# The first RMSNorm's gains: one row spread by TensorE in place of a 128-partition load, and a new order of the opening steps

## The reference

```python
def rms_norm(x, g):
    x32 = x.astype(jnp.float32)
    y = x32 * lax.rsqrt(jnp.mean(x32 * x32, axis=-1, keepdims=True) + EPS)
    return (y * g.astype(jnp.float32)).astype(x.dtype)

def reference(x, norm_mix_g, w_in, ...):
    h = x
    for layer in range(DEPTH):
        hn = rms_norm(h, norm_mix_g[layer])
        h = h + hybrid_mixer(hn, w_in[layer], ...)     # z = hn @ w_in first
        hn = rms_norm(h, norm_ffn_g[layer])
        h = h + swiglu(...) if layer % 2 == 0 else h + moe_swiglu(...)
    return rms_norm(h, final_g)
```

## Time and profile before

| | us |
|---|---|
| median of 3 runs | 2067.91 (2066.62 to 2069.62) |
| profiled execution, whole time | 2069.79 |
| its span | 2068.1 |
| PE busy | 2014.9 (97%) |
| DVE busy | 1539.8 (74%) |
| ACT busy | 1202.7 (58%) |
| POOL busy | 96.7 (5%) |

### The profile page before, as it was taken

The page is one execution under the profiler, slowest core; times in us unless marked ns, Lnnn a source line. Parts: engine busy times, 40 slices in busy tenths (PEclk is TensorE's granted clock), DMA queues, the critical chain, the costliest instruction groups (busy, mean ns, idle before and its releaser), DMA issues.

```text
span 2068.1 us, 33621 instructions
## 1 busy us (share of the span) xinstructions
PE 2014.9 (97%) x11091; PEld 1748.2 (85%) x11092; DVE 1539.8 (74%) x1705; ACT 1202.7 (58%) x1546; POOL 96.7 (5%) x142
## 2 busy tenths in 40 slices
PE   8999999999999998999999999999999999999996
PEld 7777888888888777999899988888999888889995
DVE  6896766666668976766577688898776798997774
ACT  4443555555555333655465577787655687876661
POOL 1000000100000002100000000000000000001010
PEclk9999999999999998999999999999999999999998
DMA  7321776766643313877587699999877799999771
GB/s 223 120 72 47 223 219 202 218 197 190 185 143 123 112 71 103 275 236 234 204 273 253 196 360 377 357 394 353 288 254 245 278 388 357 388 356 360 258 254 41
DMA packets 245272, 487.51 MB, mean 236 GB/s; under 512 B 16724, under 2 KB 86468, under 8 KB 245220
## 3 DMA queue, kind: packets, MB, share of 16 engines
q1 hardware_dynamic: 237668, 462.04, 66.1%
q0 software_dynamic: 7552, 24.80, 3.4%
HBM read 473.21 MB, written 13.58 MB: 235 GB/s over the span
## 4 chain that ended last, share of the span: by engine, by line
PE 82%; DVE 9%; issue 3%; DMA 3%; ACT 2%; POOL 0%; DVEq 0%; SPq 0%; ACTq 0%; POOLq 0%
PE PS L1575 81%; DMA raw<-in_expert_w 2%; DVE PS L894 2%; DVE wlo L753 2%; ACT whi L375 1%; DVE OV L868 1%; DVE OV L882 1%; PE PS L1903 1%; PE PS L1605 0%; DVE OV L898 0%; DVE OV L864 0%; PE PS L1827 0%; DMA OV<-in_norm_mix_g 0%; DMA OV<-x_tok,idx 0%; DMA raw<-in_w_in 0%
## 5 line engine op out<-in xcount | busy, mean ns | idle before, releaser
L753 DVE TENSOR_TENSOR wlo<-raw,whi 128x1024 fp32r<-128x1024 f32 x872 | 1031.9, 1221 | 201.8 <-ACT whi L375 195.9
L375 ACT ACTIVATE whi<-raw 128x1024 fp32r<-128x1024 f32 x872 | 888.0, 1053 | 255.5 <-PE PS L1575 155.9
L1575 PE MATMUL PS<-XN,whi 128*128 128x512 f32 (+3 forms) x3328 | 953.5, 363 | 15.1 <-issue 9.7
L1575 PE MATMUL PS<-XN,wlo 128*128 128x152 f32 (+3 forms) x2944 | 775.3, 263 | 1.0 <-issue 1.0
L1575 PEld LDWEIGHTS PS<-XN,whi 128*128 128x128 f32 x3328 | 618.7, 189 | 81.6 <-issue 17.5
L1575 PE MATMUL PS<-whi,XN 128*128 128x512 f32 x2272 | 672.5, 394 | 7.1 <-issue 2.2
L1575 PEld LDWEIGHTS PS<-XN,wlo 128*128 128x128 f32 x2944 | 561.9, 191 | 12.8
L1575 PEld LDWEIGHTS PS<-whi,XN 128*128 128x128 f32 x2272 | 424.5, 188 | 102.3 <-issue 6.9
L1575 PE MATMUL PS<-wlo,XN 128*128 128x512 f32 x1248 | 425.0, 392 | 0.0
L1575 PEld LDWEIGHTS PS<-wlo,XN 128*128 128x128 f32 x1248 | 234.7, 188 | 50.8
L587 ACT ACTIVATE OV<-PS 128x352 f32<-128x352 f32 x112 | 51.5, 461 | 107.8 <-PE PS L1575 107.8
(11 more groups left out here) (248 smaller groups left out, 991.6 us busy)
## 6 DMA issues: line engine op xcount, KB each, us to landing
raw<-in_expert_w SPq DMA_DIRECT2D x672, 512.0 KB, 5.1
raw<-in_ffn_w SPq DMA_DIRECT2D x144, 512.0 KB, 3.8
raw<-in_w_in SPq DMA_DIRECT2D x40, 512.0 KB, 5.4
raw<-in_w_out SPq DMA_DIRECT2D x16, 512.0 KB, 4.3
y_rows<-OV POOLq DMA_DIRECT2D x13, 512.0 KB, 4.8
y_rows<-OV POOLq DMA_DIRECT2D x13, 192.0 KB, 5.1
RES<-in_x SPq DMA_DIRECT2D x4, 512.0 KB, 5.5
x_tok<-OV POOLq DMA_DIRECT2D x4, 512.0 KB, 2.9
```

The source lines that it names most:

```text
L375: act.activation(whi[:, u0 % CONV, half(h)], raw[:, r, half(h)], ACT.Copy).then_inc(s["hi_done"], 1)
L753: dve.tensor_tensor(wlo[:, w, half(h)], raw[:, u0 % RAW, half(h)], whi[:, w, half(h)].bitcast(F32), ALU.subtract).then_inc(s["lo_done"], 1)
L1575: return pe.matmul(out_, lhsT, rhs, start=start, stop=stop, skip_group_check=True)
```

## The change

- The gains of the first norm are no longer loaded into 128 partitions by SP. ACT, as its first instruction, issues a DMA of the single 4 KB row into partition 0 of `OV` (`g_row`). TensorE multiplies a row of ones with it, twice 512 columns, into banks 2 and 3 of PSUM (`gB0`), and raises `gB0_ok`. `scaled` reads `gB0` from PSUM for the first four blocks.
- TensorE's first fillers wait for `bd_zero` 3 (the third POOL constant, `ones`) in place of `const_ok`; they multiply `ones` by `ones`. The two spreading matmuls stand behind them.
- The scratch of the four first `squares` moves from PSUM banks 0 to 3 to SBUF (`sq` and the old place of `gB`), and the wait for `ss_done` 4 ahead of the second fillers is gone. These are 20 fillers now, where 14 were.
- ACT: `squares(3)` moves behind the two halves of unit 0.
- DVE: `scaled(2)` moves from ahead of `x_lo(0)` to behind the split of the second weight half, and `scaled(3)` to between the halves of unit 1.

```diff
+        g_row = OV[0:1, 3072:4096]
+        gB0 = PS[:, 2:4, :].rearrange("p a n -> p (a n)")
@@ SP
                 sp.dma_start(RES[:, b, :], x[0, b * P:(b + 1) * P, :]).then_inc(s[f"x{b}"], 16)
-                if b == 1:
-                    sp.dma_start(gB, norm_mix_g[0].partition_broadcast(P)).then_inc(s["gB0_in"], 16)
@@ ACT
+            act.dma_start(g_row, norm_mix_g[0:1, :]).then_inc(s["gB0_in"], 16)
             act.wait_ge(s["small_ok"], 3)
@@ ACT start_norm
-                for b in range(TB):
+                def first_squares(b):
+
                     act.wait_ge(s[f"x{b}"], 16)
-                    squares(b, PS[:, 2 * (b % 2):2 * (b % 2) + 2, :].rearrange("p a n -> p (a n)"))
-                for h in range(2):
-                    x_hi(h)
-                    split(0, 0, 0, (h,))
+                    squares(b, gB if b % 2 else sq.rearrange("p c n -> p (c n)"))
+
+                for b in range(TB - 1):
+                    first_squares(b)
+                x_hi(0)
+                split(0, 0, 0, (0,))
+                x_hi(1)
+                split(0, 0, 0, (1,))
+                first_squares(TB - 1)
                 split(1, 0, 0)
@@ DVE scaled, start_norm
-                dve.scalar_tensor_tensor(x_home(n), RES[:, n % TB, :], SM[:, 40 + n:41 + n], gB, ALU.mult,
-                                         ALU.mult).then_inc(s["xt_done"], 1)
+                dve.scalar_tensor_tensor(x_home(n), RES[:, n % TB, :], SM[:, 40 + n:41 + n], gB0 if n < TB else gB,
+                                         ALU.mult, ALU.mult).then_inc(s["xt_done"], 1)
                 mean(0)
-                dve.wait_ge(s["gB0_in"], 16)
+                dve.wait_ge(s["gB0_ok"], 1)
                 scaled(0)
-                for n in (1, 2):
-                    mean(n)
-                    scaled(n)
-                for h in range(2):
-                    x_lo(h)
-                    split(0, 0, (h,))
+                mean(1)
+                scaled(1)
+                mean(2)
+                x_lo(0)
+                split(0, 0, (0,))
+                x_lo(1)
+                split(0, 0, (1,))
                 mean(3)
+                scaled(2)
+                split(1, 0, (0,))
                 scaled(3)
-                split(1, 0)
+                split(1, 0, (1,))
@@ TensorE mixer(0)
-                    pe.wait_ge(s["const_ok"], 1)
-                    keep_busy(10, 6)
+                    pe.wait_ge(s["bd_zero"], 3)
+                    for _ in range(10):
+                        mm(PS[:, 6, 0:P], ones[:, :], ones[:, :], True, True)
+                    pe.wait_ge(s["gB0_in"], 16)
+                    for h in range(2):
+                        ins = mm(gB0[:, 512 * h:512 * h + 512], ones[0:1, :], g_row[:, 512 * h:512 * h + 512], True, True)
+                    ins.then_inc(s["gB0_ok"], 1)
                     x_T(0, 0)
                     x_T(0, 1)
-                    pe.wait_ge(s["ss_done"], TB)
-                    keep_busy(14, 3)
+                    keep_busy(20, 0)
                 pe.wait_ge(s["xlo_done"], 8 * l + 2)
```

2 lines of the change are left out of this document (1 added, 1 removed).

## The result

The changed kernel took **2073.05 us** (median of 9 runs, 2067.8 to 2078.3), the kernel before 2067.91 us beside it (9 runs, 2065.05 to 2070.82). The ratio is 1.0026, with a 95% interval of 1.0015 to 1.0037. The change costs about 5 us; the prediction of 2068.0 us, with a range up to 2071.0, was wrong.

A forecast was written before the change was run, and what follows sets the result against it. The prediction took TensorE's matmul stream, hanging on the start of the first product, to bound the kernel. It summed +0.1 at S, -1.4 from the order and +1.4 from longer fillers to +0.1: 2068.0 us, range 2065.8 to 2071.0.

The forecast's parts named there:

- The change touches nothing behind the first 25 us: Whole kernel: only the opening chain up to the first product was followed; later code was taken as unaffected.
- Part 1: Opening up to block 0's scaling: the wait for the gains' load becomes a wait for fillers and spreading, +0.1 us.
- S: Start of `scaled(0)`, the scaling of block 0: forecast 7.8 us, against 7.74 before.
- wholly at the lower level: Upper bound for S: the spreading matmuls run at TensorE's lower clock and take twice as long, S = 9.7 (+1.9).
- The margin of 0.3 us: Opening on TensorE: 4.4 us of dense first fillers barely outlast the 4.1 us the clock rise took before.
- Part 2: From S to Z: data ready at S + 7.3, but 40 filler instructions hold the product until S + 8.8.
- Z: Start of TensorE's first product: forecast 16.6 us, against 16.51 before.
- the level falls back: Rival: TensorE's clock drops between spreading and second fillers, half of which run slow; +2.1 us, 2070.0, chance 0.10.
- The worth of the order: ACT and DVE opening: the reordering alone brings the data for the first product 1.4 us earlier.
- A shift of Z is carried to the end nearly one to one: From the first product to the kernel's end: every later link hangs on Z, so its shift reaches the total.
- Part 3: Opening: PSUM operands, SBUF scratch, moved scalings, weight splits and queues cost nothing, being covered by slack.
- the late clock: Rival: spreading, transposes and second fillers start at the lower clock; +4.1 us, 2072.0, at worst +6.3, chance 0.09.

The follow-up runs named there:

- before_long16: The kernel before with 16 more matmul instructions of 8 columns in the idle time ahead of its first fillers; 2072.08 us, ratio 1.0022.
- after_wide: The changed kernel with its 40 second filler instructions of 128 columns replaced by 20 of 256; 2068.97 us, ratio 1.0002.
- bridge: The changed kernel with its second fillers dealt out, some ahead of each block's transposes; 2071.10 us, ratio 1.0009.
- fill14: The changed kernel with 14 second fillers (28 instructions) in place of 20; 2069.12 us, ratio 1.0008.
- fill0_pad80: The changed kernel without second fillers, with 80 empty TensorE instructions added in three places; 2067.27 us, ratio 0.9996.
- fill0: The changed kernel without any second fillers; 2065.53 us, ratio 0.9992 to the kernel before.
- gains_only: The changed kernel with the old order on ACT and DVE and 28 second filler instructions; 2070.10 us, ratio 1.0010.
- again: The changed kernel without an edit, run again for a second trace; 2071.52 us, ratio 1.0018.
- again3: The changed kernel without an edit, a fourth look at its opening; 2070.96 us in its one run.
- again4: The changed kernel without an edit, run beside the two padded kernels; 2073.40 us, ratio 1.0025.
- order_only: The kernel before with only the new order on ACT and DVE and the scratch in SBUF, gains by the old load; 2067.34 us, ratio 1.0000.
- spread_first: The changed kernel without first fillers, spreading once the gains' row lands, 8 filler instructions behind it, 16 as second fillers; 2064.54 us, ratio 0.9985.
- lean: The same as `spread_first`, without its second fillers; 2066.49 us, ratio 0.9992 to the kernel before.
- before_pad32: The kernel before with 32 empty instructions ahead of TensorE's first wait; 2069.04 us, ratio 1.0001.
- after: The changed kernel itself, in its first measurement and trace; 2073.05 us, ratio 1.0026.
- again2: The changed kernel without an edit, a third look at its opening; 2073.97 us in its one run.

## Why the prediction was wrong

**"The change touches nothing behind the first 25 us", and "nothing else in the change can pay".** This is the step that failed. It is true of what the code computes and waits for, and false of where the code lies. 32 instructions more moved the stall near 836 by 11 matmuls, to the entry of a loop, and made it longer, from about 1.0 to 3.2 us; the stretch went from 186.7 to 190.8 us or more. `before_long16` shows that this alone gives 4.6 us (2.7 to 6.4) where the change loses about 5, and `after_wide` that without it 1.5 us (-1.4 to 2.5) is left. The stall stood in the chain of before as 0.97 us of "issue" in the midst of a dense stream, at a row that waits for nothing; the prediction didn't read that far.

**Part 1, S.** Forecast 7.8, measured 7.63, 7.57, 7.70 and 8.13 in four traces: right by each term. First filler at 1.55 (1.5), 4.13 us of fillers (4.4), spreading 1.98 us (1.88), and the product of one row costs nearly what the product of 128 rows does. In the fifth trace of this kernel S was 9.91, by the bound "wholly at the lower level" (9.7). The chance of 0.09 for that case was too small: it is one in five traces of the changed kernel, and of the six other kernels that open with the same instructions four (`bridge`, `fill14`, `after_wide`, `fill0_pad80`) show it and two (`fill0`, `gains_only`) don't. The margin of 0.3 us between 4.4 us of fillers and a rise at 4.1 us was named; and the first fillers show how thin it was: their 20 instructions took 3.91 to 4.20 us where the rise came within them, and 4.62 where it came behind. A margin like that should have had a chance near a half.

**Part 2, S to Z.** Forecast S + 8.8, measured S + 10.7. The second fillers did hold the product, and it waited for nothing else, as forecast. What was off is the duration: the fillers began 0.8 later (S + 5.2 instead of 4.35) since the transposes took twice as long, and went on for 1.1 longer (5.56 us up to the product instead of 4.46), since the lower level lasted up to 15.3. That is the rival "the level falls back", put at +2.1 with a chance of 0.10: it came at +1.85, and `again`, `again3` and `again4` show Z at 17.5 to 18.5 as well. The prediction gave beside it a sentence of the Trainium skill, in TensorE: Matmul & The Clock Gate, section Part 4: PE-mode transpose, that a transpose is no activity like a matmul. The fall doesn't need it: in the changed kernel it lies between 8 and 9, in the idle time ahead of the first transpose at 9.06. Whether the transposes made the low level last longer, no run here shows.

**The worth of the order.** Forecast -1.4, given back by the fillers. Between two kernels whose product waits for data, the old order (`gains_only`) has it at S + 8.76 and the new one (`fill0`) at S + 8.0: 0.8 us, where 1.4 was forecast. The term that was mis-sized is the transposes of block 0, taken at 1.06 us and 1.94 in `fill0`; the old order doesn't wait for them. `order_only` shows nothing in the total.

**"A shift of Z is carried to the end nearly one to one."** Up to 800 us this held. The first matmul on `tri` behind the router (it makes the lists of the experts' rows) in before, `spread_first` and `after_wide`, whose Z is 16.51, 14.51 and 20.53:

```profile
801.27 0.41 PE L1575 MATMUL PS<-OV,tri 128*128 128x32 f32 x2 [1.01 <-DVE OV L1282]
```

```profile
798.87 0.41 PE L1585 MATMUL PS<-OV,tri 128*128 128x32 f32 x2 [1.01 <-DVE OV L1292]
```

```profile
804.66 0.41 PE L1585 MATMUL PS<-OV,tri 128*128 128x32 f32 x2 [1.02 <-DVE OV L1292]
```

It stands 784.8, 784.4 and 784.1 us behind Z, and in 17 of the 20 traces between 784.1 and 784.8. The other three (`lean`, `fill0`, `fill0_pad80`) begin the product at the lower level and have 786.0 to 787.3. What failed is that one trace stood for the kernel. Z of the kernel before is 16.51 and 19.16 in its two traces and 17.45 in `before_pad32`, 17.7 on average; the changed kernel's five traces average 18.4. So the opening costs some 0.7 us of the 5, an estimate from these eight traces. The medians alone can't show a shift of 1 to 3 us: their intervals reach some 2 us to either side, and behind 806 the traces scatter by more (from the first split to the end 1259.7 to 1268.8 us in the five of the changed kernel). Between the `tri` matmul and that split some of a shift can also be lost or made: `after` had Z 1.85 later, 1.40 of it left at `tri` and 0.33 at 806; why is open.

**Part 3** held: no TensorE wait between the first products, `scaled(2)` at 16.69 and `scaled(3)` at 19.01 in good time. **The chances**: the 0.07 for slower by over 0.2% rested on the late clock and on the spread of the runs; what came, by another mechanism, was slower by 0.26%.

## What to carry to other kernels

An instruction added to a long program is not paid for where it stands alone: in the chain of the kernel before, look for short pieces of "issue" inside a dense stream, above all a few instructions behind the entry of a loop or a branch, since these are places that move when code ahead grows or shrinks, and try fillers as fewer and wider instructions. When what counts is an opening of some us that rests on TensorE's level, one trace shows one of several openings; take two or three before costing anything by its rows. And a step on which all else waits belongs ahead of the work that is meant to bring the clock up, even when it then runs at half rate: 3.75 us begun at 2.41 beat 1.98 us begun at 5.61.

## What the runs showed of the hardware

- A stall of TensorE with no open wait of the program behind it, at a fixed place of its instruction stream behind a loop's entry: four matmuls more ahead moved it four matmuls forward, 16 more put it at the entry and made it 2.8 to 3.4 us instead of 0.8 to 1.1. It ended 2.5 to 3.4 us behind the entry in all fifteen traces that have it. A stall of about 1 us cost nothing in the stretch, one of 3 us cost about 4 with what the lower level behind it adds (granted clock 0.59, 0.57).
- 16 float32 matmul instructions of only 8 columns took 3.56 us, 0.22 each, as long as those of 128 columns at the lower level.
- A one-row contraction of 512 columns took 1.98 us for four at the upper level and 3.75 to 3.78 at the lower.
- Empty instructions on TensorE (32, 80) leave the count of the page unchanged, and 32 of them left the stall where it was.
- The level fell while TensorE was idle: 0.72 from 8 to 9 in the changed kernel, with no instruction of TensorE in that window.
- The start of the first product (14.51 to 20.53) was carried one to one up to 800 us: 784.1 to 784.8 us in the 17 traces whose product begins at the upper level.
- The granted clock column reads 1.00 in stretches ahead of its first recorded change even where matmuls run at half rate; in the first microseconds the durations of a known instruction tell the level, not the column (`again2` reads 1.00 from 8 to 9, within the spreading that took 3.78 us).
- The load that spreads a row of 4 KB over 128 partitions landed at 7.7 to 9.2 us in the traces with the old way; the plain load of the row had landed at 2.41.
